# Differential attention in the order 3, 0, 1, 2 with two sets of PSUM banks, and four smaller edits

## What is computed

```python
def diff_attention(q, k, v, ...):        # block 1: 8 heads, each with two halves of 64 features
    q, k = partial_rope(q, pos), partial_rope(k, pos)
    s = where(pos_k <= pos_q, q @ k.T * 64 ** -0.5, neg)       # per half
    pr = softmax(s)
    o = (pr[half 0] - lam * pr[half 1]) @ v                    # 128 wide values
    return rms_norm(o, subln_w, 1e-5) * (1 - lambda_init)

def nsa_attention(q, k, v, gates, rel_bias):   # block 2: per head a window branch, a selected branch
    return sum(gate_b * (masked_softmax(q @ k_b.T * 0.125 + bias, mask_b) @ v_b) for b in range(3))   # and a compressed one (31 keys)

out = x * rsqrt(mean(x * x) + 1e-6) * g_final_3    # the last norm, after block 3's MLP was added to x
```

## Time and profile before

| | us |
|---|---|
| median of 3 runs | 3665.03 (3663.76 to 3668.27) |
| the profiled execution | 3664.28 |
| its span, first to last instruction | 3662.5 |
| PE busy in it | 3359.4 (92%) |
| DVE, ACT, POOL busy | 2023.8, 1230.1, 212.6 |

### The profile page before, as it was taken

The page is one execution under the profiler, slowest core; times in us unless marked ns, Lnnn a source line. Parts: engine busy times, 40 slices in busy tenths (PEclk is TensorE's granted clock), DMA queues, the critical chain, the costliest instruction groups (busy, mean ns, idle before and its releaser), DMA issues. The chain is left out here.

```text
span 3662.5 us, 57266 instructions
## 1 busy us (share of the span) xinstructions
PE 3359.4 (92%) x24193; PEld 2748.0 (75%) x24193; DVE 2023.8 (55%) x3286; ACT 1230.1 (34%) x2142; POOL 212.6 (6%) x174
## 2 busy tenths in 40 slices
PE   7988999988999999888999998979699889999998
PEld 6988888856888887656677776857578587878886
DVE  4885564564355344577546776356736545464342
ACT  4552323254333233214433222234412234333231
POOL 2323230010000000000000000000100020000000
PEclk9998998998999999999999999989799789999999
DMA  4431103101222222620122222312022003232221
GB/s 148 154 134 57 43 23 111 58 1 58 98 92 92 98 92 75 158 61 13 47 81 92 86 87 92 102 52 95 11 92 95 1 2 110 79 106 98 95 95 57
DMA packets 99462, 287.84 MB, mean 79 GB/s; under 512 B 19738, under 2 KB 23962, under 8 KB 97160
## 3 DMA queue, kind: packets, MB, share of 16 engines
q1 hardware_dynamic: 93104, 269.43, 21.6%
q10 hardware_dynamic: 6104, 14.75, 1.6%
HBM read 264.22 MB, written 19.89 MB: 78 GB/s over the span
## 5 line engine op out<-in xcount | busy, mean ns | idle before, releaser
L240 PE MATMUL acc<-h_hi,whi 128*128 128x512 f32 x1992 | 800.3, 402 | 64.8 <-DVE wlo L432 42.4
L240 PE MATMUL acc<-h_hi,wlo 128*128 128x512 f32 x1992 | 791.3, 397 | 0.0
L240 PE MATMUL acc<-h_lo,whi 128*128 128x512 f32 x1928 | 770.0, 399 | 0.0
L240 PEld LDWEIGHTS acc<-h_hi,whi 128*128 128x128 f32 x1992 | 379.1, 190 | 175.3 <-DVE wlo L432 44.7
L338 DVE TENSOR_TENSOR wlo<-wbuf,whi 128x1024 fp32r<-128x1024 f32 (+3 forms) x277 | 318.6, 1150 | 273.4 <-ACT whi L256 271.1
L240 PEld LDWEIGHTS acc<-h_hi,wlo 128*128 128x128 f32 x1992 | 379.3, 190 | 87.9
L240 PEld LDWEIGHTS acc<-h_lo,whi 128*128 128x128 f32 x1928 | 366.7, 190 | 86.1 <-issue 2.9
L256 ACT ACTIVATE whi<-wbuf 128x1024 fp32r<-128x1024 f32 (+3 forms) x277 | 274.5, 991 | 348.1 <-PE acc L240 318.3
L240 PE MATMUL acc<-arena_round,whi 128*128 128x512 f32 x736 | 236.4, 392 | 4.8 <-DVE arena_round L398 4.8
L338 DVE TENSOR_TENSOR wlo<-ahead,whi 128x1024 fp32r<-128x1024 f32 (+3 forms) x132 | 152.3, 1154 | 139.9 <-ACT whi L256 139.2
L256 ACT ACTIVATE whi<-ahead 128x1024 fp32r<-128x1024 f32 (+3 forms) x132 | 131.4, 995 | 174.1 <-PE acc L240 167.7
(11 more groups left out here) (752 smaller groups left out, 6349.4 us busy)
## 6 DMA issues: line engine op xcount, KB each, us to landing
wbuf<-in_mlp_out SPq DMA_DIRECT2D x46, 512.0 KB, 3.3
wbuf<-in_mlp_in SPq DMA_DIRECT2D x45, 512.0 KB, 3.2
wbuf<-in_w_gates SPq DMA_DIRECT2D x38, 512.0 KB, 3.3
wbuf<-in_ffn_up SPq DMA_DIRECT2D x29, 512.0 KB, 3.2
wbuf<-in_w_qkv SPq DMA_DIRECT2D x22, 512.0 KB, 3.3
rwkv_factors<-factors SPq DMA_DIRECT2D x8, 1320.0 KB, 4.6
ahead<-in_mlp_in SPq DMA_DIRECT2D x19, 512.0 KB, 3.2
wbuf<-in_w_rwkv SPq DMA_DIRECT2D x18, 512.0 KB, 5.5
```

Source lines behind the costliest of these rows:

```text
L240: mm = nc.tensor.matmul(acc[t % NB][:, 0:T], wt[s % ring][:, k - a, :], xt, start=(kx == 0 and q == 0), stop=(kx == job.K - 1 and q == 2))
```

## The change

1. diff_attention: the blocks of a head come as 3, 0, 1, 2 (`BLOCKS`). `place` puts unit 0 of a head (block 3) over both banks, unit 1 (block 0) into bank 0, unit 2 (block 1) into bank 1, unit 3 (block 2, 400 keys) into bank 0. Scores wait for the reduce that last read their bank. `swaps` of the next head uses bank 1 and comes right after the scores of unit 3 on PE; rope comes between maxima and weights of that unit on DVE. Slots are units now, four per head.
2. The 16 meta columns are made once for all heads: `metas` (8 transposes, 8 matmuls of 16 columns), 8 small products on POOL, `rope_meta` (2 operations on DVE). L1607, L1613 and L1689 go.
3. Both attentions: the reduce takes the minimum of the negated, scaled scores (`least`); `low` goes, the exponential has scale -1.0. In nsa_attention ACT does turned_weights(p - 2) and write before powers(p).
4. The last norm is folded into the last job (`Ending`): squares and sums with the tiles, x scaled by the weight in place, one ones-matmul, then eight products with the root, six on DVE and two on POOL, and the stores.
5. The first slab of the gates chain is loaded by diff_attention's SP; `ahead` is allocated at the program's start. The DMA scratch is set to 8192.

```diff
@@ chain @@
+                if ending is not None:
+                    for k in range(8):
+                        if k in by_dve_last:
+                            sp.wait_ge(last_normed, by_dve_last.index(k) + 1)
+                        else:
+                            sp.wait_ge(last_pool, 1 if k == 3 else 2)
+                        sp.dma_start(ending.dst[:, k, :], ends_on[k]).then_inc(last_stored, 16)
...
+                    for k in (3, 6):
+                        nc.gpsimd.tensor_tensor(ends_on[k], ends_on[k], scale[:], ALU.mult).then_inc(last_pool, 1)
...
+                    pe.wait_ge(summed, sum_no[S][1])
+                    nc.tensor.matmul(stat[0][:, 0:T], ones[:], sums[0][:], start=True, stop=True).then_inc(stat_ready, 1)
...
+                    if f is ending:
+                        copy(sums[0][:] if n == 0 else sqx[n % 2][:], x, ACT.Square).then_inc(sq_done, 1)
+                        copy(x, x, ACT.Copy, scale=f.cols[:, n:n + 1]).then_inc(scaled, 1)
+                        return
...
+                    TS(scale[:], stat[0][:, 0:T], 1.0 / (8 * P), ending.eps, ALU.mult, ALU.add).then_inc(var_ready, 1)
+                    dve.wait_ge(root_ready, no)
+                    nc.vector.reciprocal(scale[:], scale[:]).then_inc(scale_ready, 1)
...
+                    for k in by_dve_last:
+                        TT(ends_on[k], ends_on[k], scale[:], ALU.mult).then_inc(last_normed, 1)
@@ diff_attention @@
+        BLOCKS = (3, 0, 1, 2)
+        def place(e, a):
+            start = (LO, 0, BANK, 0)[a % NJ]
+            return ps_s[e][:, start:start + keys(a)]
...
+                sp.dma_start(ahead.place[:], following[0, 0]).then_inc(ahead.loaded, 16)
...
+                def metas():
+                    for i in range(8):
+                        mm = nc.tensor.transpose((ps_t, ps_m)[i // 4][0:M, i % 4 * P:(i % 4 + 1) * P], p[i + 16][:, 0:M], c["ident"][:])
+                    mm.then_inc(vtm_ready, 1)
+                    for i in range(8):
+                        mm = nc.tensor.matmul(ps_s[1][:, M * i:M * (i + 1)], c["rope_swap"][:], p[i + 8][:, 0:M], start=True, stop=True)
+                    mm.then_inc(meta_swap, 1)
...
                     for e in range(2):
-                        h = slice(64 * e, 64 * e + 64)
-                        nc.tensor.matmul(ps_s[e][:, LO:BANK], r[h, 0, j * P:(j + 1) * P], r[h, 1, 0:M], start=True, stop=True)
-                    for e in range(2):
-                        h = slice(64 * e, 64 * e + 64)
-                        nc.tensor.matmul(ps_s[e][:, BANK:LO + keys(a)], r[h, 0, j * P:(j + 1) * P], r[h, 1, M:keys(a)],
-                                         start=True, stop=True).then_inc(sc_ready[e], 1)
+                        h, to = slice(64 * e, 64 * e + 64), place(e, a)
+                        q = r[h, 0, b * P:(b + 1) * P]
+                        free = a if a % NJ < 2 else a - 1
+                        if free > 0:
+                            pe.wait_ge(least_ready[e], free)
+                        nc.tensor.matmul(to[:, 0:M], q, meta[h, i, :], start=True, stop=True)
+                        nc.tensor.matmul(to[:, M:keys(a)], q, r[h, 1, 0:keys(a) - M], start=True, stop=True).then_inc(sc_ready[e], 1)
...
+                for a in range(NA + 3):
+                    if a < NA:
+                        scores(a)
+                    if a < NA - 1 and a % NJ == NJ - 1:
+                        swaps(head(a) + 1)
+                        values(head(a) + 1)
+                    if 2 <= a < NA + 2:
+                        turn(a - 2)
+                    if a >= 3:
+                        weigh(a - 3)
...
-                        nc.vector.tensor_tensor_reduce(out=sc[e][a % 2][:, 0:n], in0=ps_s[e][:, LO:LO + n], in1=c["mask128"][:, T1 - n:T1],
-                                                       scale=1.0, scalar=NEG, op0=ALU.add, op1=ALU.max,
-                                                       accum_out=top[e][:, a:a + 1]).then_inc(top_ready[e], 1)
-                    for e in range(2):
-                        dve.wait_ge(top_ready[e], a + 1)
-                        TS(low[e][:, a:a + 1], top[e][:, a:a + 1], -SCALE, None, ALU.mult).then_inc(max_ready[e], 1)
+                        nc.vector.tensor_tensor_reduce(out=sc[e][a % 2][:, 0:n], in0=place(e, a), in1=c["mask128"][:, T1 - n:T1],
+                                                       scale=-SCALE, scalar=-NEG, op0=ALU.add, op1=ALU.min,
+                                                       accum_out=least[e][:, a:a + 1]).then_inc(least_ready[e], 1)
@@ nsa_attention @@
                 for p in range(NP + 7):
-                    if p < NP:
-                        powers(p)
                     if 2 <= p < NP + 2:
                         turned_weights(p - 2)
                     if p >= 6 and (p - 6) % 3 == 2 and p - 6 < NP:
                         write((p - 6) // 3)
+                    if p < NP:
+                        powers(p)
```

More of the change, by code:

```diff
@@ L147, in chain @@
         fold_job[s] = slabs[s - 1][0]
+    ending = next((f for _, f in folds if isinstance(f, Ending)), None)
+    ends_on = jobs[-1].dst
+    by_dve_last = (0, 1, 2, 4, 5, 7)
     two_norms = any(f.inner is not None for f in stat_at.values())
@@ L329, in _ @@
                     act.wait_ge(arrived, 16 * len(loads))
+                if ending is not None:
+                    act.wait_ge(var_ready, len(stat_at) + 1)
+                    copy(scale[:], scale[:], ACT.Sqrt).then_inc(root_ready, 1)
             @block.vector
@@ L1650, in weigh @@
                         pe.wait_ge(o_copied, a)
-                    nc.tensor.matmul(ps_o[:, 0:P], wTm[a % 2][:], vtm[i][:], start=True, stop=False)
+                    nc.tensor.matmul(ps_o[:, 0:P], wTm[a % 2][:], vtm[:, head(a), :], start=True, stop=False)
                     for b in range(n):
@@ L1787, in _ @@
                 chain(TS(neg_lam[:], neg_lam[:], -LAMBDA_INIT, None, ALU.add))
-                for i, a, a1, _, _ in lagging():
-                    if a is not None:
+                rope(0)
+                rope_meta()
+                for a in range(NA + 1):
+                    if a < NA:
                         maxima(a)
-                    elif i is not None:
-                        rope(i)
-                    if a1 is not None:
-                        weights(a1)
+                    if a < NA - 1 and a % NJ == NJ - 1:
+                        rope(head(a) + 1)
+                    if a >= 1:
+                        weights(a - 1)
                 chain(nc.vector.reciprocal(inv[:], total[0][:]))
@@ L2110, in nsa_attention @@
         wT = [[s.sb("wT", [P, TN, P]) for _ in range(2)] for _ in range(2)]
-        top, low = ([s.sb(n, [P, NP]) for _ in range(2)] for n in ("top", "low"))
+        least = [s.sb("least", [P, NP]) for _ in range(2)]
         total, share = s.sb("total", [P, NG, 6]), s.sb("share", [P, NG, 6])
@@ L2229, in powers @@
                         at = 3 * e + PLACE[br]
-                        act.wait_ge(max_ready[e], p + 1)
-                        copy(b, b, ACT.Exp, bias=low[e][:, p:p + 1], accum_out=total[:, g, at:at + 1]).then_inc(exp_ready[e], 1)
+                        act.wait_ge(least_ready[e], p + 1)
+                        copy(b, b, ACT.Exp, scale=-1.0, bias=least[e][:, p:p + 1], accum_out=total[:, g, at:at + 1]).then_inc(exp_ready[e], 1)
                 def turned_weights(p):
```

247 lines of the change are left out of this document (98 added, 149 removed).

## The result

The changed kernel takes 3643.41 us (median of 4 runs, 3639.59 to 3650.21) against 3666.65 for the kernel before in the same series; the ratio is 0.9939, 95% interval 0.9926 to 0.9952. It is faster, as forecast, by 23 us where 36 were forecast: 3643.4 lies above the forecast of 3628 and just above the range, whose upper end was 3642. Run once more beside other kernels it took 3643.35. The profiled execution has a span of 3638.6 (before 3662.5) and took 3640.57.

A forecast was written before the change was run, and what follows sets the result against it. PE was taken as busy 3359.4 of 3662.5 us, so gains lie where it waits: 14 (differential attention) + 11 (second block) + 3.3 (early load) + 8 (norm) = 36.3 off 3664.3, giving 3628; range 3614 to 3642.

The forecast's parts named there:

- the part on the differential attention: Differential attention, 732 to 864 us: new block order and shared meta columns take about 14 us less, bounds 6 and 20.
- Lag 0.8 for a stretch of low clock somewhere: Differential attention: a term of 0.8 us within the stage's sum of about 14 us less.
- rival c: PE fills up: clock stays high at both starts, heads take 12.8 us, the whole 3616; chance 0.08.
- The head: Differential attention, one steady head: 13.7 us for 15.13, 1.4 less, over heads 1 to 6 8.6 us.
- rival (a): Differential attention: the halves' score matmuls no longer overlap or a wait blocks; head 14.8 us, the whole 3637; chance 0.13.
- Second block: Second block's attention: ACT copies wT before the exponentials and 96 lows go, 9.7 + 1.3 = 11 us less; bounds 3 and 16.
- Rival (b): Second block's attention: DVE takes over or PE's wait moves to the exponentials; part gives 3 us, whole 3636; chance 0.12.
- Early load: Start of the gates chain: first weight slab loaded during the attention, ACT starts with SP, 3.3 us less; low end 2.5.
- Final norm: Kernel's end: norm work hides under the last tiles and the end comes 8.0 us earlier; bounds 6.5 and 8.5.
- so some loss is sure, but the stores cover 1.6 us of it: Final norm's last products: DVE slows beside POOL (0.92 us for 0.63 at 400 columns), but the stores cover 1.6 us.
- an end 1.1 us later: Final norm: if DVE and POOL block each other fully, the eight products take 6.3 us and the end comes 1.1 later.
- Rival (d): Both attentions: the reduce with negative scale and min is no longer one pass; three times as long gives 3716; chance 0.03.

The follow-up runs named there:

- the gap filled: Changed kernel plus three one-pass matmuls of 512 columns on idle data behind the 144-key scores in heads 2 to 8: 3620.11 us, ratio 0.9875.

## Why the prediction was wrong

**The step that failed** is in the part on the differential attention: "Lag 0.8 for a stretch of low clock somewhere". That term was 0.8 us less, and in the first trace the falls cost 22.1 in the heads and 1.0 behind them. The prediction gave the clock two ways to go, the same or better (rival c, "PE fills up: the clock stays high"), on the thought that a PE that waits less holds its clock better. The runs say otherwise. The old loop waits 2.05 us of each head and lost its clock in one of the last six heads of the traced execution, the new one waits 0.75 and lost it in four of six; a loop that the profile shows without any wait lost it too (96 columns in the gap), and one with 0.3 us per head did not (512 columns).

What the runs show in the place of that step: in the new loop the clock hangs on what stands in the gap behind the scores of 144 keys. All 25 falls start at its end or up to 2.2 us behind, wide matmuls in it end them, thin ones don't, and wide ones elsewhere don't. Why the new loop falls there and the old one, with a wait of 0.61 us in the same place and more waits besides, does not, stays open. So the rows of the old loop could not have told of the falls. But they showed its first head at half clock (0.53 in rows 1), and a price for losing more of the clock belonged in the range.

**The head** was sized right: 13.87 for 13.7, one PE wait of 0.75 for 0.9, DVE's waits 1.06 and 1.26 us ahead of 272 and 400 keys for 1.0 and 1.3, the first head shorter too. With the gap filled the stage to the gates chain took 137.5 for 159.4 before, 21.9 less where 14 + 3.3 had been forecast. The 4.6 beyond are mostly the first head, which ran at full clock in that execution. In the traces in which its clock fell too, the stage took 140.0 and 141.1, 19.4 and 18.3 less.

**The halves' overlap**, rival (a), did not come: the records of both halves start within 0.1 us of each other where PE doesn't wait for one of them (760.83 and 760.93 above), and four records of 512 columns take 1.11 us (1.14 before).

**Second block**: 13.6 for 11. The place was right, the size too small, because I let only the third units' waits (9.7) count and put the second units' 4.7 beside a busy DVE. All of PE's waits for wT, 15.3 us, vanished, and the order alone made the stage 13.9 us shorter. The lows were forecast at 1.3 and measured 1.0 to 1.3. Rival (b) did not come: DVE is busy 101 of 141.

**Early load**: 3.3 forecast; ACT begins with SP, and PE 1.8 us after the last output is scaled where it took 5.1: 3.3. No second wait followed, PE waits only once in the first 16 us of that chain.

**Final norm**: 5.7 for 8.0. The working up to the first store holds (forecast 8.0 less, measured 16.7 - 8.8 = 7.9). The failed term is "so some loss is sure, but the stores cover 1.6 us of it". The loss was priced by a row in which POOL cost 0.3 us (0.92 for 0.63); here the second and the third DVE product took 1.07 more each. The Trainium skill ("SBUF — State Buffer", section on rules for kernel authors) has it that a DVE operation with two SBUF inputs and a POOL operation that reads SBUF block each other fully, the later one until the first is done. That fits this trace: 0.69 for the DVE product that starts first, then 1.75 and 1.75 us beside POOL's 1.76 and 1.70. What I had worked out from it, an end 1.1 us later, was nearer than the sum; measured were 2.0.

**Rival (d)** did not come: the minimum over 528 keys takes 0.71 us as the maximum did.

**The 4.3 us ahead of the attention** are, as far as the runs tell, luck of this execution and were in neither sum. Without them the changed kernel's trace is 19.6 us ahead of the other: 36.3 - 18.5 (attention and load) + 1.5 (the chain behind them) + 2.6 (second block) - 2.3 (norm) + 0.1. The 18.5 are the 23.1 by which this stage (160.6) is longer than with the gap filled (137.5), 22.1 in the heads and 1.0 behind them, less the 4.6 by which 137.5 lies under the forecast of 142.1. Of these 4.6 the first head at full clock makes 2.5 to 3.6, by the two traces in which it fell.

## What to carry to other kernels

A loop in which PE waits less does not by that keep TensorE's clock: here falls that cost 22 us ate a gain of 1.3 us per head. So when a stage of many small matmuls is reordered, put a price on a lost clock into the range, and read the granted clock head by head in the result. If it falls, find out what stands just ahead of the falls in several traces, and try a wide matmul on idle data in that gap: one of 512 columns brought 20 us here, six of 16 columns nothing, and three of 512 in another place cost time. On the last stretch of a kernel, where each product releases a store, compare the products on one engine with a split: two of eight on POOL made the end 2.0 us longer here.

## What the runs showed of the hardware that I had not expected

- TensorE's clock fell to half with PE busy all of the time by the profile: 58.93 of 58.93 us at a mean granted clock of 0.68. The same loop with one matmul of 512 columns in the gap instead of the small ones, and 0.3 us of idle time per head, kept it at 1.00 for 83.21 us.
- In six traces with a wait of 0.75 us open in each head, all 25 falls of the heads 2 to 8 started from 0.1 us ahead of the end of that wait to 2.2 us behind it.
- A fall of 10.2 or 13.7 us cost this loop 4.7 or 6.3 us, nearly half its length. The second block's attention got two falls in the one run with ACT's old order and minima (PE's busy time 146.5 for 136.4) and none behind its start in any other trace, the kernel before with its longer waits included; why is open.
- Two-input products of 512 columns on DVE took 1.75 us when they started while a POOL product of 1.7 us ran, 0.68 without: the POOL operation cost DVE its own length, less the 0.6 that it lay beside the DVE product before.
